# Two-layer hybrid diffusion step on eight cores: first loads regrouped, adaLN weight turns moved, the first FFN block of each layer widened to three slabs, and the second mixer's last norm run over into the FFN

## The reference

```python
def modulate(x, g, shift, scale):
    return rms_norm(x, g) * (1 + scale) + shift

def gmlp_mixer(h, w_in, v_g, w_s, b_s, w_out):
    u, v = jnp.split(jax.nn.gelu(h @ w_in), 2, axis=-1)
    v = rms_norm(v, v_g).reshape(B, nc, CHUNK, GMLP_GROUPS, GMLP_GROUP_DIM)
    s = jnp.einsum('gts,bnsgc->bntgc', w_s, v) + b_s.T[:, :, None]
    return (u * s.reshape(B, T, GMLP_WIDTH)) @ w_out

def conv_ffn(h, w_up, conv_w, w_down):
    z = dwconv3(h @ w_up, conv_w)
    g, val = jnp.split(z, 2, axis=-1)
    return (jax.nn.silu(g) * val) @ w_down

# per layer, for context tokens xp and latent tokens xs
sh, sc, gt, sh2, sc2, gt2 = split(silu(cond) @ ada_w[l] + ada_b[l])
x = x + gt * mixer(modulate(x, norm_mix_g[l], sh, sc))
x = x + gt2 * conv_ffn(modulate(x, norm_ffn_g[l], sh2, sc2), w_up[l], ffn_conv_w[l], w_down[l])
```

## Time and profile before

| | |
|---|---|
| median of 3 runs | 1246.74 us (1243.68 to 1292.15) |
| the profiled execution's own time | 1240.95 us |
| its span, core 3, the slowest | 1239.4 us (all cores 1228.0 to 1239.4) |
| PE busy | 1143.4 us, 92% |
| DVE / ACT / POOL busy | 58% / 48% / 31% |
| granted TensorE clock, mean of core 3 | 0.972 |
| DMA queues: POOL's / SP's share of 16 engines | 49.4% / 3.8% |

### The profile page before, as it was taken

The page is one execution under the profiler, slowest core; times in us unless marked ns, Lnnn a source line. Parts: engine busy times, 40 slices in busy tenths (PEclk is TensorE's granted clock), DMA queues, the critical chain, the costliest instruction groups (busy, mean ns, idle before and its releaser), DMA issues.

```text
span 1239.4 us, 23439 instructions; the slowest of 8 cores (1228.0 to 1239.4 us)
## 1 busy us (share of the span) xinstructions
PE 1143.4 (92%) x7803; PEld 653.6 (53%) x7803; DVE 714.6 (58%) x1294; ACT 599.8 (48%) x1023; POOL 380.3 (31%) x480
## 2 busy tenths in 40 slices
PE   1478889998999999999999999998799999999998
PEld 0244454455555555555656655555355565555565
DVE  1356654535559887118797105355789951599921
ACT  3457443567587554006885027433686630356600
POOL 2233210001247443003574004335465420244310
PEclk9689899999999999999999999999899999999999
DMA  9981266584347993323673590120069838258234
GB/s 192 174 200 33 45 115 111 109 148 84 69 93 127 178 174 69 67 62 69 119 146 69 95 178 1 22 48 1 6 127 161 153 75 178 66 101 151 52 92 104
DMA packets 26229, 125.93 MB, mean 102 GB/s; under 512 B 3584, under 2 KB 12032, under 8 KB 14720
## 3 DMA queue, kind: packets, MB, share of 16 engines
q0 software_dynamic: 15456, 108.99, 49.4%
q1 hardware_dynamic: 10656, 15.45, 3.8%
HBM read 226.60 MB, written 6.82 MB: 188 GB/s over the span
## 4 chain that ended last, share of the span: by engine, by line
PE 82%; DMA 7%; DVE 3%; issue 3%; ACT 2%; POOL 1%; DVEq 0%; ACTq 0%; POOLq 0%; SPq 0%
PE ps_b L178 82%; DMA sinT<-sin 3%; DMA xT<-x_sb 2%; DMA ada_b<-ada_w 2%; DMA ada_f<-ada_w 1%; DVE xT L228 1%; DMA xT<-x_sa 1%; POOL uT L207 1%; ACT sq L204 1%; DVE hT L220 1%; ACT sqg L204 0%; PE ps_b L182 0%; DVE cv_m L207 0%; DVE tmg L207 0%; DVE tm L207 0%
## 5 line engine op out<-in xcount | busy, mean ns | idle before, releaser
L178 PE MATMUL ps_b<-hT,H 128*128 128x386 bf16 (+3 forms) x2816 | 484.0, 335 | 0.0
L228 DVE SCALAR_TENSOR_TENSOR tf<-ps_b,small,tf 128x384 f32<-128x384 f32 (+3 forms) x704 | 425.4, 632 | 64.7 <-ACT tf L204 23.3
L178 PEld LDWEIGHTS ps_b<-hT,H 128*128 128x128 bf16 x2816 | 275.7, 98 | 204.5 <-issue 2.1
L204 ACT ACTIVATE tf<-ps_b,small 128x384 f32<-128x384 f32 (+3 forms) x352 | 204.0, 593 | 261.4 <-PE ps_b L178 259.5
L207 POOL TENSOR_TENSOR act<-tf,tf 128x384 bf16<-128x384 f32 (+3 forms) x176 | 182.3, 1036 | 307.7 <-ACT tf L204 234.0
L178 PE MATMUL ps_b<-act,wdn 128*128 128x384 bf16 (+2 forms) x1408 | 239.4, 333 | 0.2 <-POOL act L207 0.2
L228 DVE SCALAR_TENSOR_TENSOR xT<-ps_b,modv,xT 128x384 f32<-128x384 f32 (+4 forms) x128 | 79.6, 632 | 224.9 <-PE ps_b L178 224.9
L178 PEld LDWEIGHTS ps_b<-act,wdn 128*128 128x128 bf16 x1408 | 137.3, 98 | 101.4 <-issue 0.4
L204 ACT ACTIVATE tf<-tf 128x384 f32<-128x384 f32 (+3 forms) x176 | 93.4, 532 | 14.0 <-DVE tf L228 13.4
L204 ACT ACTIVATE PT<-ps_b 128x1024 bf16<-128x1024 f32 (+2 forms) x77 | 71.8, 964 | 43.0 <-PE ps_b L178 42.5
L178 PE MATMUL ps_b<-hT,w_cj 128*128 128x452 bf16 (+2 forms) x384 | 80.7, 358 | 7.6 <-DVE hT L220 2.8
(11 more groups left out here) (145 smaller groups left out, 979.4 us busy)
## 6 DMA issues: line engine op xcount, KB each, us to landing
H<-w_up POOLq DMA_DIRECT2D x44, 1024.0 KB, 10.0
wdn<-w_down POOLq DMA_DIRECT2D x16, 1408.0 KB, 14.3
ada_b<-ada_w POOLq DMA_DIRECT2D x13, 1024.0 KB, 8.9
ada_a<-ada_w POOLq DMA_DIRECT2D x7, 1024.0 KB, 10.7
ada_f<-ada_w POOLq DMA_DIRECT2D x4, 1024.0 KB, 13.1
S<-w_in_o POOLq DMA_DIRECT2D x2, 2048.0 KB, 19.8
xT<-x_sa SPq DMA_DIRECT2D x2, 1536.0 KB, 12.8
w_cj<-w_cnv POOLq DMA_DIRECT2D x4, 768.0 KB, 12.8
```

Of the source, the lines that this page charges most:

```text
L178: return self.add("pe", lambda e: e.matmul(out.ap, lhsT.ap, rhs.ap, start=start, stop=stop, **kw), reads=[lhsT, rhs], writes=[out])
L204: return self.add("act", lambda e: e.activation(out.ap, in_.ap, func, **kw), reads=reads, writes=writes)
L228: return self.add(eng, lambda e: e.scalar_tensor_tensor(out.ap, in0.ap, sc, in1.ap, op0, op1), reads=reads, writes=[out])
```

## The change

- **First loads.** Both first x tiles are issued on SP at once, without a wait between them. The four first adaLN halves are issued on POOL in a row, the first after the tile SA0 has landed (before: the first at the start beside SA0; the second after SA0; SA1 after the first half; the third after SA1).
- **Conv slabs 1 and 2.** POOL issues them only after the third tile (`lx2`, SB) has landed.
- **adaLN turns.** In stage 1 the second turn comes after `step(None, (2, 1), 2)` instead of before it, the third one step later, the fourth is gone. In the first FFN pass a turn comes every 6 units instead of every 8.
- **First FFN block** of both layers: slabs 0, 1, 2 instead of 0, 1.
- **gMLP loop.** The norms' lag is 4 instead of 7, a slot pops two norm items per projection instead of one, SA1's norm is the light form, and what is left of it at the end is not drained there but goes into the FFN's hook, four items per unit until it is done.

```diff
-        la = ada_first(1, 0)
-        ada_first(1, 1, [lx0])
-        lx1 = P.dma("sp", xT[:, :, 385:769], dram(d_x1.ap()), after=[la])
-        ada_first(0, 0, [lx1])
+        P.dma("sp", xT[:, :, 385:769], dram(d_x1.ap()))
+        ada_first(1, 0, [lx0])
+        ada_first(1, 1)
+        ada_first(0, 0)
         ada_first(0, 1)
...
         for j in range(1, 3):
-            P.dma("pool", w_cj[j].whole(), dram(cnv_src[:, j]))
+            P.dma("pool", w_cj[j].whole(), dram(cnv_src[:, j]), after=[lx2] if j == 1 else ())
...
         v_units(hT, 771, 6, 3, 2)
+        step(None, (2, 1), 2)
         ada_stage1()
-        step(None, (2, 1), 2)
         need("p")
...
         run_side(99)
+        step((hT, PP, 2, None), (1, 2))
         ada_stage1()
-        step((hT, PP, 2, None), (1, 2))
         P.dma("pool", w_cj[1].whole(), dram(cnv_src[:, 3]))
         step((hT, PP, 3, None), (0, 2))
         step((h_sx, SX, 4, 1152))
-        ada_stage1()
...
-            blocks = [[0, 1]] + [[t] for t in range(2, NHS)] if first_outer else [[t] for t in range(NHS)]
+            blocks = [[0, 1, 2]] + [[t] for t in range(3, NHS)] if first_outer else [[t] for t in range(NHS)]
...
-            if n % 8 == 2 and (ada_in or ada_ld):
+            if n % 6 == 2 and (ada_in or ada_ld):
                 ada_turn()
...
-            return norm_list(1, 1, toks, xT, hT, sqg, rss, tmg, hbases, light, lag=7)
+            return norm_list(1, 1, toks, xT, hT, sqg, rss, tmg, hbases, light, lag=4)
...
-        nga = lambda: ng.extend(n2_list([SA1], [rsg[0]], [385]) + [lambda: dup(770, 768)])
+        nga = lambda: ng.extend(norm_list(1, 1, [SA1], xT, hT, sqg, [rsg[0]], tmg, [385], True, lag=4)
+                                + [lambda: dup(770, 768)])
...
                     if fill:
                         fill.popleft()()
-                    if ng:
-                        ng.popleft()()
+                    for _ in range(2):
+                        if ng:
+                            ng.popleft()()
...
         for f in op_items(slabO, uT, SA0, 1):
             f()
-            for _ in range(2):
+            for _ in range(3 if len(ng) > 18 else 1):
                 if ng:
                     ng.popleft()()
-        while ng:
-            ng.popleft()()
-
-
+
+
+        fq.extend(ng)
+        n_left = [len(ng)]
...
         def hook10(n):
-            for _ in range(1 + n % 2):
-                if fq and n >= 1:
+            for _ in range(4 if n_left[0] > 0 else 1 + n % 2):
+                if fq:
                     fq.popleft()()
+                    n_left[0] -= 1
+            assert n < 5 or n_left[0] <= 0
```

More of the change, by code:

```diff
@@ L1351, in build @@
             f()
-            for _ in range(2):
+            for _ in range(3 if len(ng) > 18 else 1):
                 if ng:
                     ng.popleft()()
-        while ng:
-            ng.popleft()()
+        fq.extend(ng)
+        n_left = [len(ng)]
+        print('LEFT', len(ng))
         fq.extend(n2_list([SA0], [rsg[1]], [C_SA], light=True))
         def hook10(n):
-            for _ in range(1 + n % 2):
-                if fq and n >= 1:
+            for _ in range(4 if n_left[0] > 0 else 1 + n % 2):
+                if fq:
                     fq.popleft()()
+                    n_left[0] -= 1
+            assert n < 5 or n_left[0] <= 0
         def store(o, tok):
```

## The result

The changed kernel takes 1260.56 us (median of 4 runs, 1259.13 to 1262.17), the kernel before 1247.43 on the same chip. The ratio is 1.0125, 95% interval 1.0104 to 1.0147: some 15.6 us slower by the ratio, 13.1 by the two medians, and 1260.56 lies just over the upper end of my range (1232 to 1260). Ratios leave out the slow executions, in which the cores of one die show a lower granted clock throughout, as in the one of 1292.15 us. The profiled execution took 1262.17 us (span 1260.6, core 0), 21 us more than that of before.

The account below looks back on a forecast made before the run. PE, holding 82% of the chain, was taken to bound the kernel through its waits and the clock drop behind them. Terms summed to +2.2 us on 1240.95, 1243.2; plus 3 for the median, 1246 us; range 1232 to 1260.

Parts of the forecast that it names:

- Start, -2: First loads and conv slabs: 4 us won on `w_qkv`, SB's wait gone, against a POOL hold; sum -2 us (-6 to +5).
- Second turn, -0.5: Stage 1's second adaLN turn: its 4.44 us wait goes, but PE then waits for DVE; -0.5 us (-5 to +1).
- Attention's entry, -6.5: adaLN turn at the attention's entry: 3.99 us wait and some 2.5 of slow clock go; -6.5 us (-7 to -3).
- Layer 0's wide block, +6.2: Layer 0's three-slab first FFN block: PE waits 4.2 us for slab 2, plus 2 of clock; +6.2 us (+3 to +8).
- gMLP ring, +7.6: End of gMLP loop, engines waiting in a circle: added DVE norm items delay the last `uT` 5.7 us; +7.6 (0 to +10).
- The sign that I named: End of the gMLP loop: PE would wait for POOL's `uT` ahead of SA0's output projections, 4 to 5 us.
- Rival 2: gMLP loop: idle DVE, POOL and ACT absorb the added norm items, so the loop costs 0; total -8.4, 1235 us; chance 0.25.
- Norm idle, -11.6: Between gMLP loop and layer 1's FFN: 8.2 us PE idle, plus slow matmuls, goes; -11.6 us (-12 to -8).
- Column 770, +3: Layer 1's FFN, seventh unit: SA1's norm that runs over is late, ACT being tight; +3 us (0 to +7).
- Slab 4 in layer 1, +6: Layer 1's first FFN pass: load issued 7.1 us behind PE, lands 9.3 later, 10.5 covered; +6 us (+2 to +9).
- Rival 1: Wide FFN blocks: two or three slabs per layer come late, landings over 12 us; +13, 1257 us; chance 0.17.
- rival 3: Start: first loads gain nothing and the POOL wait costs all 6.6 us, +5 instead of -2; total +9, 1253 us; chance 0.11.

Follow-up runs that it names:

- e2: Kernel before with only one edit: POOL issues conv slabs 1 and 2 only after tile SB has landed; ratio 1.0026 (1.001 to 1.0041).
- e1: Kernel before with only the regrouped first loads (both first x tiles at once on SP, four adaLN halves in a row on POOL); ratio 0.9997.
- e11: Kernel before with conv slabs 1 and 2 held for SB's landing, but issued on POOL behind the second of SA0's products; ratio 0.9992.
- e3: Kernel before with only the adaLN turn edits (stage 1 turns moved, fourth gone, one every 6 units in the first FFN pass); ratio 0.9984.
- e4: Kernel before with only the three-slab first FFN block, in layer 0 alone; ratio 1.0124 (1.0071 to 1.0176).
- e14: The whole changed kernel timed once more against the kernel before; ratio 1.0109 (1.0084 to 1.0134).
- e6: Kernel before with only the three-slab first FFN block, in layer 1 alone, all norms drained ahead of the FFN; ratio 1.0133 (1.011 to 1.0157).
- e15: Changed kernel with two-slab first blocks in both layers, against the kernel before: +7.9 us on each die's middle core, +6.2 and +4.4 on the slowest.

## Why the prediction was wrong

**Start, -2: it measured +3 to +4.5** (the ratio of e2, and the middle cores of its dies)**.** Three steps of this term failed. I took 4 us off the landing of `w_qkv`; e1 shows less than 1. On that rested "SB lands at about 62.7" and the product 2.2 us late; in the changed kernel SB lands at 67 (56.95 + 10.0) and the product stands at 69.70 for 62.72, 7.0 us late. My upper end said just that (SB at 67, the product 6.6 late). And I took one core for all: the 3.29 us wait that I credited stands on core 3 of the kernel before, while four of its eight cores have no such wait above 1 us; the hold on POOL costs every core. e11 shows that even without POOL's hold nothing is to be had.

**Second turn, -0.5: as said.** The 4.44 us wait goes and PE waits for DVE instead.

**Attention's entry, -6.5: about -2.** The wait went, as said, and the clock gave 1.9 for 2.5. "Nothing else is late there" was wrong: DVE's `modv` is, by 1.34 us. The turn moved to the FFN costs 0.8 where I put 0. And the attention as a whole is 1.7 us longer in the median, of which the 1.34 is a part (over all profiles, medians of 158.6 to 160.6 us with this edit and 157.6 to 159.0 without); where the rest comes back differs by core, and I did not settle it.

**Layer 0's wide block, +6.2: about right.** The pass is 148.5 us for the 141.2 that it takes with the turns alone (e3): +7.3. Slab 2 is right: 4.90 us of wait for 4.2, 2.0 of clock for 2 (5.18 for 3.2). Slab 4, which I put at 0 with an end of +5, is waited for 0.93 us on core 0, and not at all on four cores. My landing of 9.3 us held for it: the first slab of a bunch of three lands in 7.5 to 10.6 us, and the second and third, which take 12 to 24, are not needed sooner. Alone (e4) the block costs more, +9 and up to +16 by core, and there a turn's load just ahead of the bunch has its share.

**gMLP ring, +7.6: right in size, not in its parts.** From the loop's first matmul to the end of the last `uT` product before, 755.3 to 865.4, are 110.1 us; after, 765.4 to 882.6, 117.2: +7.1 where the sum had 5.7, and no slow clock behind it where the sum had 1.9 (the 60 matmuls of the output projections take 9.96 us before and after). The sign that I named is not there: PE waits for `uT` 0.88 and 0.30 us ahead of SA0's projections, 0.88 and 0.38 before. The wait of 4 to 5 us is there, 6.35 us between 869.6 and 882.76 for 1.69 before, but for `vn` (2.39) and for SB's squares (2.16), whose norm now stands ahead of the product. The two added table loads cost as in the earlier trace rows, 1.28 us each, with the next operation at most 1.30 behind their start. Rival 2, that the ring takes the items in, falls. **Norm idle, -11.6: right**, 22.1 us from the first output projections behind that product to the FFN before (865.5 to 887.65), 11.1 after (882.76 to 893.88): -11.0, and some 1.7 of clock in the first units.

**Column 770, +3: 4.3** (2.54 of wait, 1.8 of clock: 4.47 for 2.63); on cores 1, 3 and 5 there is no slow clock behind the wait.

**Slab 4 in layer 1, +6: about 12.** The wait was computed right, step by step. POOL's lag is 7.2 us (the twelfth unit ends near 931.2, the issue is at 938.41), the landing 9.8, the cover 10.5: 6.5, and 6.53 are measured. What failed is that I charged no clock behind it, though I had said 2 us for each such wait. It was 5.4 here (79.07 for 73.6), partly at half clock and partly at 0.81; on cores 4, 5 and 6 of the same profile 2.4.

By terms then: start +5 to +6 over the forecast, attention and turn +4 to +5, layer 0 +1, layer 1 +3 by the medians of the stages and +7 on the profiled core. All large errors point the same way. The clock weighs as much as the waits: by the page PE's busy time grew from 1143.4 to 1155.5 us for the same 7803 matmuls, +12.1, and its idle time from 96.0 to 105.1, +9.1. So my last sign, a change of PE's waits by more than 10 us, did not come, and the forecast fell all the same. Some 8.5 of the 12.1 are 45.3 us at 0.81 (an estimate, 0.19 of them), two thirds of it in layer 0's second pass; whether the change brings those about stays open (e14).

Rival 1 (starved for slabs, 1257) was the nearest in time, but by luck: its price was slabs late by 11 us more than I had summed, at a landing of over 12 us, and in the changed kernel the slabs that are waited for land in 7.5 to 10.6. What failed is rival 3's step (the start is lost), the entry to the attention, and the clock behind slab 4.

## What to carry to other kernels

- A block that keeps several weight buffers in use must issue each next load right behind the last read of the buffer that it takes. Issued at the block's end, they leave the queue idle (24 us in e6) and come late; the same block with issues in place cost nothing (140.4 us for 149.6).
- A landing time holds for a load's place in the queue. Of three slabs that left together the first landed in 9.8 us, the second in 15.8, the third in 22.7; and behind a turn's load that had left 3.9 us earlier the first took up to 13.8.
- Read a wait on all cores before you credit its end. The profile's slowest core can have a wait that half of the others lack.
- Never make an engine that computes wait for a DMA in order to hold back another one, unless nothing behind the waiting instruction is due; and charge the clock behind every PE wait that you add; behind one that you remove, look for what is late next before you credit anything.

## What the hardware showed beyond that

- **A granted clock of 0.81 with PE busy throughout.** It is neither of the two levels, and on the second die of e15's chip it stretched a pass from 118.0 to 123.0 us. The Trainium skill (TensorE: Matmul & The Clock Gate, "Seeing it yourself") has a peak-current limiter that takes a whole die to 13/16 of the clock once three of its cores run dense matmuls. 13/16 is 0.81, so the level agrees. The rest does so in part. The stretches last 4 to 15 us at a time, in passes of 118 us. They come by pairs of cores: 0 and 1, 2 and 3, and so on show the same ones, and the two pairs of a die differ. And on four chips, in fourteen profiles, eight cores ran such passes at 1.00 throughout, so as a figure to plan with it is not borne out. Cores 1 and 2 of e14, one die, in the same pass:

```profile
622.00:627.00 5.00, 5.00 (x32) 3.01 (x31) 4.58 (x9) 4.12 (x10) 3.81 (x6) 1.00 0.71 128
...
622.00:627.00 5.00, 5.00 (x27) 2.74 (x26) 4.58 (x10) 4.11 (x10) 3.81 (x6) 0.81 0.77 123
```

- **Two queues share the engines.** SB's 1.58 MB from SP took 20.1 us beside three loads on POOL's queue and 9.1 to 10.3 us on the eight cores of the changed kernel, where those loads are held back. The Trainium skill (DMA: Bandwidth & Descriptors, "Queues, rings and completion order") says that each engine goes round the queues that have work; these landing times agree with it. But with the same three loads behind it the tile landed in 8.7 to 10.5 us on cores 2, 4 and 6 of the kernel before; why the loads did not slow it there, no run shows.
- **The cores are not alike in landing.** In e4 the same slab 2 is waited for 2.6 to 2.8 us on cores 0, 3, 5 and 7 and 4.1 to 5.4 us on the others. It is one core of each pair (0 and 1, 2 and 3, ...), the one that issues first: in e4, the changed kernel and e14 its slab lands in 7.5 to 8.6 us, that of the other in 8.9 to 10.4, in all twelve pairs. Why the second of a pair gets its slab later, no run here shows.
